# Seam columns and other queue orders in the projection stage of a hybrid encoder kernel

## What is computed

```python
xn = rms_norm(x, norm1)
proj = xn @ w_in                         # [hyena x0, x1, v | q | k | v]
uc = short_conv(proj[..., :1536], conv_w, conv_b)   # width 3, centred: needs both neighbour rows
x0, x1, v = jnp.split(uc, 3, axis=-1)
h_f, h_b = implicit_filter(L, ...)       # two sine layers over position features, times a decay
y_hy = x0 * bidir_long_conv(x1 * v, h_f, h_b, hy_skip)     # rfft, product, irfft at 2L
y_at = window_gqa(q, k, v, ...)          # |q-k| <= 128
h = x + concat(rms_norm(y_hy), rms_norm(y_at)) @ w_out
y = h + (silu(gate) * up) @ w_down       # gate, up = rms_norm(h) @ w_gate_up
```

## Time and profile before

| what | value |
| --- | --- |
| median of 3 runs | 2722.42 us (2719.92 to 2726.14) |
| the profiled execution | 2725.49 us, span 2723.7 us |
| TensorE matmuls, weight loads | 96%, 88% of the span |
| DVE, ACT, POOL | 77%, 50%, 45% |
| granted TensorE clock, mean | 0.987 |

### The profile page before, as it was taken

One profiled execution on the slowest core, in us unless ns is written; L12 is line 12 of the kernel. 1 busy time (PEld: TensorE's weight loads), 2 busy tenths in 40 slices (PEclk: granted clock), 3 DMA queues, 4 the chain that ended last, 5 costly groups with the idle time before them and its releaser, 6 DMA issues.

```text
span 2723.7 us, 39433 instructions
## 1 busy us (share of the span) xinstructions
PE 2614.8 (96%) x13881; PEld 2388.3 (88%) x13881; DVE 2105.7 (77%) x2508; ACT 1371.5 (50%) x2365; POOL 1233.3 (45%) x1182
## 2 busy tenths in 40 slices
PE   8899999899998999999999999999999989999998
PEld 6888889888896888878999999899999989999997
DVE  6765664688548777867888888988888898888887
ACT  5564544477437787764434434443434443443432
POOL 1655211112212444465677854455654444444443
PEclk9999999999998999999999999999999999999999
DMA  7687967899986464454444443543333354332332
GB/s 231 198 278 227 315 211 220 279 276 282 266 215 178 130 151 125 122 165 150 136 140 138 140 121 112 194 141 115 113 110 104 93 182 157 92 93 89 90 90 89
DMA packets 470044, 446.33 MB, mean 164 GB/s; under 512 B 54670, under 2 KB 377358, under 8 KB 469559
## 3 DMA queue, kind: packets, MB, share of 16 engines
q1 hardware_dynamic: 441960, 372.22, 47.1%
q0 software_dynamic: 27888, 71.58, 8.4%
HBM read 329.90 MB, written 113.79 MB: 163 GB/s over the span
## 4 chain that ended last, share of the span: by engine, by line
PE 83%; DVE 8%; DMA 3%; issue 2%; ACT 2%; SPq 2%; POOL 0%; DVEq 0%; ACTq 0%; POOLq 0%
PE ff_banks L85 17%; PE ff_banks L86 17%; PE ff_banks L87 17%; PE pr_acc L85 4%; PE pr_acc L86 4%; PE pr_acc L87 4%; PE am_mix L85 2%; PE am_mix L86 2%; PE am_mix L87 2%; DMA sp_k<-k_dram 2%; PE am_turn L2310 2%; PE pr_gen L85 1%; PE pr_gen L87 1%; PE pr_gen L86 1%; PE am_acc L2324 1%
## 5 line engine op out<-in xcount | busy, mean ns | idle before, releaser
L3445 DVE TENSOR_TENSOR ff_h<-ff_h,ff_banks 128x1536 f32<-128x1536 f32 x231 | 402.9, 1744 | 5.7 <-PE ff_banks L87 5.2
L3281 ACT COPY ff_r<-ff_banks 128x384 f32<-128x384 f32 x198 | 94.9, 479 | 590.2 <-PE ff_banks L87 590.1
L3428 DVE TENSOR_TENSOR ff_dlo<-ff_dlo_raw,ff_dhi 128x512 fp32r<-128x512 f32 x231 | 213.0, 922 | 172.7 <-ACT ff_dhi L3311 172.6
L85 PE MATMUL ff_banks<-ff_xhi,ff_ghi 128*128 128x384 f32 x924 | 313.5, 339 | 12.3 <-DVE ff_silu L3405 6.5
L85 PE MATMUL pr_acc<-pr_xhi,pr_whi 128*128 128x386 f32 (+1 forms) x864 | 304.7, 353 | 16.2 <-DVE pr_xlo L1639 16.2
L87 PE MATMUL ff_banks<-ff_xhi,ff_glo 128*128 128x384 f32 x924 | 311.6, 337 | 0.0
L85 PE MATMUL ff_banks<-ff_xhi,ff_uhi 128*128 128x384 f32 x924 | 310.8, 336 | 0.6 <-ACT ff_r L3281 0.6
L86 PE MATMUL ff_banks<-ff_xlo,ff_ghi 128*128 128x384 f32 x924 | 311.2, 337 | 0.0
L86 PE MATMUL ff_banks<-ff_xlo,ff_uhi 128*128 128x384 f32 x924 | 310.6, 336 | 0.0
L87 PE MATMUL ff_banks<-ff_xhi,ff_ulo 128*128 128x384 f32 x924 | 310.0, 335 | 0.0
L3129 POOL TENSOR_TENSOR ff_act<-ff_act,ff_silu 128x384 f32<-128x384 f32 x99 | 117.1, 1183 | 418.1 <-issue 235.5
(11 more groups left out here) (351 smaller groups left out, 6678.6 us busy)
## 6 DMA issues: line engine op xcount, KB each, us to landing
ff_glo_raw<-w_gate_up SPq DMA_DIRECT2D x132, 256.0 KB, 3.0
ff_ulo_raw<-w_gate_up SPq DMA_DIRECT2D x132, 256.0 KB, 2.9
ff_dlo_raw<-dsum_dram SPq DMA_DIRECT2D x132, 256.0 KB, 2.7
pr_raw<-w_in SPq DMA_DIRECT2D x108, 256.0 KB, 5.7
ff_dlo_raw<-w_down SPq DMA_DIRECT2D x99, 256.0 KB, 2.6
sp_k<-k_dram SPq DMA_DIRECT2D x64, 256.0 KB, 5.7
pr_xs<-x SPq DMA_DIRECT2D x18, 512.0 KB, 5.9
xkeep_dram<-pr_xs SPq DMA_DIRECT2D x18, 512.0 KB, 4.7
```

Source lines behind the costliest of these rows:

```text
L85: pe.matmul(out, still[0], moving[0], start=start, stop=False, skip_group_check=goes_on)
L3281: act.copy(kept[n][:], bank(X)).then_inc(copied, 1)
L3428: dve.tensor_tensor(dlo[d_slot(n)][:], din[d_slot(n)][:], dhi[d_slot(n)][:].bitcast(F32), ALU.subtract).then_inc(d_low, 1)
L3445: dve.tensor_tensor(to, to, lowered_all(k), ALU.add).then_inc(added, 1)
```

## The change

Seven parts.

1. The seam. For rounds 1 to 5 two columns are written apart: the last of tile 2 and the first of tile 3 (`SEAM` = 384 and 385), by two small ACT copies and two small DVE subtractions (`seam`), from the turned rows in `xs`. Tile 2 is then written without its last column and tile 3 without its first (`turned_span`), and `rows_needed` of window 0 goes from tiles 0 to 3 to tiles 0 to 2, with a wait on the count of edge columns (`edge_lows`). `turn(r, 2)` moves from behind the last half chunk of the old round to ahead of it; tile 3's transposes and copy back (`lift(r, 3)`) stay where `turn(r, 2)` was, with the seam behind them. The zero columns of rounds 2 and 5 are written with `turn(r, 3)`, not `turn(r, 2)`.
2. `norm` becomes `squares` (ACT) and `scale` (DVE), and `scale` is issued later: for tile 6r+5 (r from 1) behind `turn(r, 4)`, for tile 6r+6 behind the first window's eviction, for the next four behind the second half chunk of window 1.
3. `wave_end(0, 1)` is issued ahead of `wave_mid(1, 1)`.
4. The prompt's two tiles of gated input come by one load into a buffer of their own (`prompt_u`), issued with the first two of the ring; the ring serves the other sixteen.
5. The first two octets are split in two slots of their own (`octet_parts`), ahead of `product_step(2)`.
6. Between `first_z` and `z_parts` there are two more empty slots.
7. SP's wait before it refills tile 2's place in the ring of rows counts two more for rounds 1 to 5.

After the change `product_step(2)` is in slot 146, `z_step(0)` in 187, `z_step(15)` in 217 (213 before), `opening` in 219 to 222. The diff, cut:

```diff
+    def turned_span(r, j):
+        a, b = (0, P) if r == 0 or j not in (2, 3) else ((0, P - 1) if j == 2 else (1, P))
+        return slice(a, b), slice(place(r, j) + a, place(r, j) + b)
+    def edge_lows(r, seam=True):
+        return sum((0, 1, 3, 2, 1, 3)[k] + 2 for k in range(1, r + 1)) - 2 * (not seam)
...
         for r in range(ROUNDS):
             end = units_of(r) - 1
-            turn(r, 2)
             if r:
+                lift(r, 3)
+                seam(r)
                 evict(r - 1, units_of(r - 1) - 1, 1)
                 yield
+            else:
+                turn(0, 2)
             turn(r, 3)
             if r == 0:
                 norm(GT - 2)
-            norm(GT * r + GT - 1)
+            squares(GT * r + GT - 1)
             if r:
                 yield
+            else:
+                scale(GT - 1)
...
                 if i == 0:
                     turn(r, 4)
+                    if r:
+                        scale(GT * r + GT - 1)
                     if r < ROUNDS - 1:
-                        norm(GT * r + GT)
+                        squares(GT * r + GT)
                 yield
                 if i == 0:
                     turn(r, 5)
                 second_half(r, i, 0)
                 evict(r, i, 0)
+                if i == 0 and r < ROUNDS - 1:
+                    scale(GT * r + GT)
                 if i == 0 and peeks(r):
                     turn(r, 6)
...
                 first_half(r, i, 1)
                 if 1 <= i <= 4 and r < ROUNDS - 1:
-                    norm(GT * r + GT + i)
+                    squares(GT * r + GT + i)
                 if i == end and r < ROUNDS - 1:
                     turn(r + 1, 1)
                 yield
+                if i == end and r < ROUNDS - 1:
+                    turn(r + 1, 2)
                 second_half(r, i, 1)
+                if 1 <= i <= 4 and r < ROUNDS - 1:
+                    scale(GT * r + GT + i)
...
+    prompt_u = Place(nc, "ur", pr.end + 40960).sb("us_prompt", [P, 2, HY])
...
         wave(1, 1)
         yield
+        wave_end(0, 1)
         wave_mid(1, 1)
-        wave_end(0, 1)
...
             return_step(j - 2)
             yield
+            if j == 1:
+                for t in range(2):
+                    octet_parts(t)
+                    yield
         first_z()
         yield
         yield
+        yield
+        yield
         z_parts()
...
     # SP
-                sp.wait_ge(x_low, 2 * last_turn(n - 5) + 2)
+                sp.wait_ge(x_low, 2 * last_turn(n - 5) + (4 if (n - 5) // GT and (n - 5) % GT == 2 else 2))
...
         def bring_u(t):
+            if t >= N2:
+                return
...
             bring_u(1)
+            sp.wait_ge(weighted, NTT)
+            sp.dma_start(prompt_u[:], u_rows[LS:T].rearrange("(t p) c -> p t c", p=P)).then_inc(skip_in, 16)
...
     # TensorE
         def rows_needed(rd, c):
-            return 2 * turn_number(rd, 4 if c == 0 else GT + peeks(rd))
+            return 2 * turn_number(rd, (3 if rd else 4) if c == 0 else GT + peeks(rd))
...
                 if rd and c == 0:
-                    pe.wait_ge(edge_low, (0, 1, 4, 6, 7, 10)[rd])
+                    pe.wait_ge(edge_low, edge_lows(rd))
...
     # ACT
+        def seam(rd):
+            act.wait_ge(unit_done, 2 * first_unit(rd))
+            if rd < NG:
+                act.wait_ge(x_copied, 2 * (GT * rd + 3) + 2)
+            for s in range(2):
+                act.copy(xhi[:, :, SEAM + s:SEAM + s + 1], edge_rows(rd, s)).then_inc(edge_high, 1)
...
-            if j < NOCT:
+            if 2 <= j < NOCT:
                 octet_high(j)
...
     # DVE
-            if not peeks(rd) and j == 2:
+            if not peeks(rd) and j == 3:
                 dve.wait_ge(unit_done, 2 * first_unit(rd))
                 dve.memset(xhi[:, :, 4 * P + 1:4 * P + 2].bitcast(F32), 0.0).then_inc(edge_low, 1)
                 dve.memset(xlo[:, :, 4 * P + 1:4 * P + 2].bitcast(F32), 0.0).then_inc(edge_low, 1)
...
+        def seam(rd):
+            dve.wait_ge(edge_high, edge_highs(rd))
+            for s in range(2):
+                o = slice(SEAM + s, SEAM + s + 1)
+                dve.tensor_tensor(xlo[:, :, o], edge_rows(rd, s), xhi[:, :, o].bitcast(F32), ALU.subtract).then_inc(edge_low, 1)
...
-            if j < NOCT:
+            if 2 <= j < NOCT:
                 octet_low(j)
```

More of the change, by code:

```diff
@@ L185, in peeks, with edge_highs @@
         return r % NG < NG - 1
+    SEAM = 2 * P + P
+    def turned_span(r, j):
+        a, b = (0, P) if r == 0 or j not in (2, 3) else ((0, P - 1) if j == 2 else (1, P))
+        return slice(a, b), slice(place(r, j) + a, place(r, j) + b)
+    def edge_highs(r):
+        return sum((k != NG) + 2 for k in range(1, r + 1))
+    def edge_lows(r, seam=True):
+        return sum((0, 1, 3, 2, 1, 3)[k] + 2 for k in range(1, r + 1)) - 2 * (not seam)
     def turn_number(r, j):
@@ L231, in columns, with course, squares, scale @@
         return [(3 * HY + (HEADS + 2 * (i - 6)) * HD, P, 0)]
-    def course(now, norm_rows, weights, turn, u_turn, first_half, second_half, evict):
+    def course(now, norm_rows, scale_rows, weights, turn, lift, seam, u_turn, first_half, second_half, evict):
         UN = first_unit(ROUNDS)
-        def norm(n):
+        def squares(n):
             if n < NTT:
                 norm_rows(n)
+        def scale(n):
+            if n < NTT:
+                scale_rows(n)
+        def norm(n):
+            squares(n)
+            scale(n)
         norm(0)
@@ L861, in sync @@
         now = [0]
-        woven(course(now, nothing, weights, turn, nothing, nothing, second_half, nothing),
+        woven(course(now, nothing, nothing, weights, turn, nothing, nothing, nothing, nothing, second_half, nothing),
               side(now, wave, nothing, nothing, made_step, nothing, nothing, first_eighth, eighth,
-                   first_u, u_step, product_step, return_step, first_z, z_step, nothing, nothing, opening))
+                   first_u, u_step, product_step, return_step, first_z, z_step, nothing, nothing, nothing, opening))
         for c in range(2):
@@ L1066, in turn, with lift @@
         def turn(rd, j):
+            if rd == 0 or j != 3:
+                lift(rd, j)
+        def lift(rd, j):
             n = GT * rd + j
@@ L1350, in turn @@
             q = turn_number(rd, j)
-            if rd and j < 2:
+            if rd and j < 3:
                 act.wait_ge(unit_done, 2 * first_unit(rd) - 1)
@@ L1357, in turn @@
             n = GT * rd + j
-            if rd >= NG:
-                act.wait_ge(x_in[n % 5], 16 * (n // 5 + 1))
-            elif j < GT:
-                for h in range(2):
-                    act.wait_ge(x_turned, 2 * q + h + 1)
-                    act.copy(xs[:, n % 5, 512 * h:512 * h + 512], turned[:, h, :]).then_inc(x_copied, 1)
+            if (rd >= NG or j < GT) and (rd == 0 or j != 3):
+                lift(rd, j)
             for h in range(2):
@@ L1373, in turn, with lift @@
                 else:
-                    act.copy(xhi[:, 4 * h:4 * h + 4, place(rd, j):place(rd, j) + P], got).then_inc(x_high, 1)
+                    t, o = turned_span(rd, j)
+                    act.copy(xhi[:, 4 * h:4 * h + 4, o], got[:, :, t]).then_inc(x_high, 1)
+        def lift(rd, j):
+            n, q = GT * rd + j, turn_number(rd, j)
+            if rd >= NG:
+                act.wait_ge(x_in[n % 5], 16 * (n // 5 + 1))
+                return
+            for h in range(2):
+                act.wait_ge(x_turned, 2 * q + h + 1)
+                act.copy(xs[:, n % 5, 512 * h:512 * h + 512], turned[:, h, :]).then_inc(x_copied, 1)
+        def seam(rd):
[4 more added lines that the diff above has]
+                act.copy(xhi[:, :, SEAM + s:SEAM + s + 1], edge_rows(rd, s)).then_inc(edge_high, 1)
         def u_turn(e):
@@ L1600, in scalar, with scale_rows @@
         now = [0]
-        woven(course(now, norm, weights, turn, u_turn, nothing, nothing, evict),
+        woven(course(now, norm, nothing, weights, turn, lift, seam, u_turn, nothing, nothing, evict),
               side(now, wave, nothing, wave_end, made_step, weigh_step, prompt, nothing, eighth,
-                   first_u, u_step, product_step, return_step, nothing, z_step, eighth_parts, z_parts, opening))
+                   first_u, u_step, product_step, return_step, nothing, z_step, eighth_parts, z_parts, octet_parts, opening))
     def vector(dve, opening):
-        def norm(n):
+        def scale_rows(n):
             if n == 0:
@@ L1862, in vector @@
         now = [0]
-        woven(course(now, norm, weights, turn, u_turn, nothing, nothing, evict),
+        woven(course(now, nothing, scale_rows, weights, turn, nothing, seam, u_turn, nothing, nothing, evict),
               side(now, wave, wave_mid, wave_end, made_step, weigh_step, nothing, nothing, eighth,
-                   first_u, u_step, product_step, return_step, first_z, z_step, eighth_parts, z_parts, opening))
```

(1 more changed line is left out.)

34 lines of the change are left out of this document (23 added, 11 removed).

## The result

The changed kernel takes 2738.31 us in the median (2735.5 to 2742.99, 4 runs), the kernel before 2722.08 us on the same chip: a ratio of 1.0059, interval 1.0045 to 1.0073. It is slower by 16 us. The forecast was 2726.1 us with a range of 2712 to 2735, so the time lies above the range.

What follows compares the result with a forecast made beforehand. TensorE, busy 96% of the span, bounds the kernel, so only its gaps and low-clock stretches can give time. Terms 4.0 - 1.2 + 4.6 + 4.1 - 0.1 - 4.2 - 5.3 + 1.8 = +3.7 us on 2722.4: 2726.1, range 2712 to 2735.

Steps and rivals of the forecast that it cites:

- round 0: Row 6 is scaled behind the first eviction, so its transposes go from 36.89 to 39.65: +4.0 us (2.7 to 4.5).
- change to round 1 and round 1: Rows scaled later make transposes wait; second window starts at 175.6, not 171.0: +4.6 us (3.1 to 5).
- round 2: Tile 5's transposes wait about 4 us for copies, subtractions and scaling: +4.1 us (2.5 to 5).
- prompt and round 4: Two early gaps go, but a filter load holds the fourth product step to 544.7: -4.2 us (-8.4 to -2).
- round 5 and inverse: Gap of 3.84 us and ACT's 5.72 us stop go; inverse's first step at 706.5: -5.3 us (-7 to -3).
- Round 3: First window starts earlier, second gains 1.6 us, but a 4.4 us idle gap costs clock: -0.1 us (-1.6 to 0).
- the handover: Start of attention: four more slots delay the opening and block 1's queries: +1.8 us (0.5 to 4).
- the filter's term: Filter's first steps: earlier first feature mostly removes a 3.5 us wait, the following wait grows: -1.2 us (-3.5 to 0).
- The early places: Signs on TensorE: later transposes in rounds 0 to 2; scaled-row waits 7.0 to about 17 us, low-part waits 16.2 to about 9.
- The clock behind the gaps: TensorE runs at half clock after a long gap, costing some 1.3 to 2.6 us; 1.3 charged in rounds 0 and 1.
- the whole 8.4: Round 4's full gain if the filter load takes 2.6 us and holds nobody; kernel would end at about 2722.
- The rival of the late output weights: Handover: output weights leave 8 to 9 us later, +4 to +8 us above the sum's tail, 2731; chance 0.18.

## Why the prediction was wrong

The table from above, with borders nearer to the forecast's terms. Lost us:

| stretch, half chunks | before, twice | after, twice | difference of means | forecast |
| --- | --- | --- | --- | --- |
| round 0, 0 to 11 | 7.7, 8.8 | 11.9, 10.5 | +3.0 | +4.0 |
| filter steps, 12 to 29 | 10.9, 9.5 | 14.3, 14.3 | +4.1 | -1.2 |
| change to round 1 and round 1, 30 to 61 | 12.8, 13.5 | 18.7, 19.0 | +5.6 | +4.6 |
| round 2, 62 to 93 | 7.9, 7.1 | 12.5, 12.3 | +4.9 | +4.1 |
| prompt and round 4, 125 to 173 | 27.5, 24.6 | 23.4, 20.2 | -4.3 | -4.2 |
| round 5 and inverse, 174 to 203 | 14.9, 12.8 | 12.1, 10.9 | -2.4 | -5.3 |

Round 3 and the handover stand as above.

The steps that failed are the filter's term, a gain of 1.2 us where 4.1 were lost, and round 5's, 5.3 us where 2.4 came; then the handover's.

**The early places were right, the filter's term was not.** Round 0's transposes of row 6 start at 39.33 us (39.6 forecast; the wait is 3.96, not 2.6), scaled rows cost 20.3 us of waiting (about 17), low parts 8.2 (about 9), round 2's sixteen transposes are split by a wait of 4.02 us, round 3 waits 4.19 us ahead of its second window, the prompt 0.98. But rounds 0 to 2 lost 17.6 us where I summed 11.5, and 5.3 of these 6.1 us are the filter's. I had a gain there because the first feature comes earlier; DVE is busy without a hole, so what arrives late stays late: TensorE's waits there are 5.38 and 2.8 us, where 3.5, 1.9 and 0.7 stood before. The size is unsure: thirteen profiles with the order of before lie at 9.3 to 12.8 us in this stretch, those with swap and late scaling at 14.3, 14.3 and, without slots, 12.7; no gain is seen in any. The share of each move stays open: the swap without late scaling lost 13.6 us there, late scaling without the swap 12.6 and 12.5.

**The clock behind the gaps was mis-sized in its place, and is a small part in all.** I charged 1.3 us to a gap near 4 us. In round 1 of the changed kernel three gaps follow each other (2.81, 2.01 and 3.46 us), and the stretch over them stands at 0.90 of the clock (length, busy us by engine, granted clock, DMA share, GB/s):

```profile
162.00:211.00 49.00, 40.72 (x197) 36.05 (x195) 27.70 (x40) 25.70 (x47) 20.01 (x31) 0.90 0.74 248
```

A tenth of 49 us is 4.9 us of clock for three gaps, where I had one gap's 1.3. In the two profiles of the kernel before the same part of round 1, 39 us, stood at 1.00 and 0.96. But over rounds 0 to 2 most of the 17.6 us is idle time: with each interval of more than 0.4 us beyond its full-clock value counted as a gap, gaps make 13.7 of it and slower matmuls 3.9, against 2.6 of clock that I charged in rounds 0 and 1.

**Round 4 came out by luck.** I fixed the fourth product step by one load of 11.22 us, and so allowed 4.2 us of 8.4; 4.3 came, but not in that way. The fourth product step starts at 562.45 in the changed kernel and waits for nothing, where I had a wait of 3.3 us. The load of 11.22 us was one execution's: the third product waited for no load in the second profile of the same kernel, nor in the changed one. Of the 4.07 us ahead of round 4's second window, which I had going, 2.96 stay, for low parts. What the prompt's early rows gain beyond that (half chunks 125 to 155 lost 7.1 us less) the later products give back. The two gaps that I counted as 7.1 us add up to 6.8 (3.51 - 0.8 + 4.07). One landing time of one execution is a draw, not a bound.
The Trainium skill (DMA: Bandwidth & Descriptors, Anatomy of one DMA) gives an estimate of 2.6 us for this load, and so the whole 8.4. That this load holds nobody was so in the changed kernel, but the loads of this kind from 550 to 600 us there took 3.7 to 8.6 us to land, 5.5 in the median, so the measured times decide against the 2.6. The page's fit is for transfers that GpSimd issues; these are issued by SP.

**Round 5 and the inverse gave 2.4 us, where I summed 5.3.** The gap for low parts and ACT's stop went, as said. In their place are 2.48 us for the last return's low part, 0.98 us ahead of the first window, 1.54 us for the inverse's rows and 2.12 us for the rows of `row_dram`. I had followed the return and the inverse's first rows to their time and counted the wait only there; the return's own matmuls wait for DVE (2.48 us) in a slot with no other work. And what did come is not the seam's, to which I gave it: the empty slots alone bring it.

**The handover cost 4.0, not 1.8.** I priced a single block's queries; the loss is there in each kernel with four slots. The rival of the late output weights did not come: in the changed kernel ACT takes the first of them at 845.44, straight behind its instruction before, without a wait for a load.

**The range.** The recorded upper end, 2735, is called the sum of the upper ends for early rounds and handover. With rounds 0 to 2 and the handover at their upper ends and the rest at its forecasts the sum is +7.7, 2730.1 us; only with every term at its upper end is it +13.5, 2735.9. The filter went beyond its end (4.1 for 0), round 1 too (5.6 for 5), and round 5 was short of its least gain (2.4 for 3). A rival in which the late gains fail was missing.

**A better version.** Parts 1, 4, 5 and 7 without late scaling, the swap and the empty slots took 0.9986 of the time before (0.9975 to 0.9998; 2717.46 us in the median): a gain of some 4 us, and 20 us under the changed kernel. Its neighbours with two or four slots lie within its interval, so that no single part of it is shown to make the gain. It is also the best of nine kernels without late scaling, and its interval ends close to 1, so the gain itself is weakly shown; the 20 us against the changed kernel are not in doubt.

## What to carry to other kernels

On an in-order engine, ask of each moved instruction who waits for it next, and not whether its engine has room. A row scaled behind an eviction is late by what stands ahead of it on DVE, the eviction and the tile's low parts, and with it all of TensorE. Price a gap with its clock, by a range and not by one number: measured here, gaps of 5.6 and 6.0 us in all lost 6.6 and 10.9. Book no gain for a removed wait until the next two waits in line have been followed to the same time; the waits removed in rounds 3 and 5 moved to the next consumer. And where an engine is busy without a hole, as DVE is at the filter, an instruction that arrives late stays late: a gain booked there needs the hole that would make room for it.

## What the hardware showed that was not expected

The price of a gap jumps, and its length alone doesn't set it. In round 1 a gap of 3.59 us left the clock at 1.00 (2.4 GHz), while one of 4.07 us at the same place, and the chain of 2.81, 2.01 and 3.46 us, gave stretches at 0.84 and 0.90. But the kernel before, profiled twice, has the same gap at the same place with both outcomes. First the one profile, then the other (TensorE's timeline, and the stretch):

```profile
160.64 1.06 PE L1078 MATMUL pr_turned<-pr_ident,pr_xs 128*128 128x128 f32 x8 [1.95 <-ACT pr_ust L1389]
...
160.00:170.00 10.00, 8.98 (x52) 7.51 (x52) 9.02 (x14) 8.57 (x20) 4.14 (x7) 1.00 0.98 340
```

```profile
161.02 1.76 PE L1148 MATMUL pr_turned<-pr_ident,pr_xs 128*128 128x128 f32 x8 [1.97 <-ACT pr_ust L1472]
...
160.00:170.00 10.00, 8.98 (x48) 8.20 (x49) 8.49 (x12) 8.61 (x19) 4.39 (x7) 0.83 1.00 332
```

And the filter's gap of 2.5 us later in round 1 stands in 10 us at 0.83 in both of these profiles, and in 10 us at 1.00 in the changed kernel (2.58 us). So two profiles with one gap each don't tell what a gap costs.

The same load from memory held DVE for 3.02 us in one execution and for none in the next, and the filter's steps, with their own instructions in the same order, lost anything from 9.3 to 12.8 us.
